# Eight early tile pairs, squares summed beside TensorE, and a new order of the token sums at the start of a feed-forward

## The reference

```python
y = jnp.concatenate([y_a, y_b, y_c, y_d], axis=-1) @ w_out[l]
x = layer_norm(ALPHA * x + g1 * y, ln1_w[l], ln1_b[l])
x = layer_norm(ALPHA * x + g2 * swiglu(x * (1.0 + sc2) + sh2, w_ffn_in[l], w_ffn_out[l]), ln2_w[l], ln2_b[l])

def swiglu(h, w_in, w_out):
    g, u = jnp.split(h @ w_in, 2, axis=-1)
    return (jax.nn.silu(g) * u) @ w_out
```

## Time and profile before

| | us |
|---|---|
| median of 3 runs | 2479.55 (2476.06 to 2481.32) |
| profiled execution | 2475.26 |
| its span | 2473.5 |
| TensorE busy | 2289.2 (93%) |
| VectorE busy | 1366.7 (55%) |
| ScalarE busy | 808.6 (33%) |
| GpSimd busy | 286.2 (12%) |

### The profile page before, as it was taken

The page is one execution under the profiler, slowest core; times in us unless marked ns, Lnnn a source line. Parts: engine busy times, 40 slices in busy tenths (PEclk is TensorE's granted clock), DMA queues, the critical chain, the costliest instruction groups (busy, mean ns, idle before and its releaser), DMA issues. The chain is left out here.

```text
span 2473.5 us, 26601 instructions
## 1 busy us (share of the span) xinstructions
PE 2289.2 (93%) x10498; PEld 1702.9 (69%) x10498; DVE 1366.7 (55%) x2048; ACT 808.6 (33%) x1359; POOL 286.2 (12%) x230
## 2 busy tenths in 40 slices
PE   6999997878969999999999989998799999898999
PEld 3444853567638888887888668985577977444887
DVE  3779538375776555555456575229646186664310
ACT  3101113533362333333433353334344332344210
POOL 0000000200133233220000000026200000021000
PEclk9999989958979999999999999999899999898999
DMA  7541029105312222225543121000222110102322
GB/s 262 159 130 34 1 58 322 39 1 170 119 34 86 90 83 84 77 73 191 190 129 129 56 86 52 26 1 26 69 65 68 35 42 27 52 19 82 99 79 60
DMA packets 210564, 210.47 MB, mean 85 GB/s; under 512 B 18658, under 2 KB 167450, under 8 KB 209512
## 3 DMA queue, kind: packets, MB, share of 16 engines
q1 hardware_dynamic: 194892, 190.51, 24.5%
q0 software_dynamic: 3664, 12.35, 1.4%
q10 hardware_dynamic: 11884, 5.91, 0.9%
HBM read 167.92 MB, written 39.64 MB: 84 GB/s over the span
## 5 line engine op out<-in xcount | busy, mean ns | idle before, releaser
L2234 PE MATMUL bk_in<-t_part,a 128*128 128x512 f32 x1320 | 313.1, 396 | 29.3 <-DVE t_part L2672 10.5
L2234 PEld LDWEIGHTS bk_in<-t_part,a 128*128 128x128 f32 x1320 | 251.6, 191 | 87.3 <-issue 16.6
L2257 PE MATMUL bk_in<-hid_part,b_part 128*128 128x512 f32 x1056 | 245.8, 394 | 7.0 <-DVE b_part L2568 7.0
L2257 PEld LDWEIGHTS bk_in<-hid_part,b_part 128*128 128x128 f32 x1056 | 200.2, 190 | 51.9 <-DVE b_part L2568 8.7
L991 PE MATMUL fr_ps<-arena,work 128*128 128x512 f32 x384 | 168.5, 600 | 5.0 <-DMA work<-in_w_in 5.0
L4204 PE MATMUL fo_ps<-fo_hi,fo_part 128*128 128x512 f32 x512 | 161.8, 394 | 10.8 <-DVE fo_lo L4248 10.8
L2995 PE MATMUL bk_in<-h_part,sj_part 128*128 128x512 f32 x576 | 136.0, 397 | 6.2 <-DVE h_part L2722 5.1
L991 PEld LDWEIGHTS fr_ps<-arena,work 128*128 128x128 f32 x384 | 73.5, 193 | 96.4 <-issue 91.2
L3437 PE MATMUL aj_ps<-h_part,aj_part 128*128 128x512 f32 x576 | 137.9, 400 | 0.0
L2995 PEld LDWEIGHTS bk_in<-h_part,sj_part 128*128 128x128 f32 x576 | 109.4, 191 | 32.8 <-issue 6.2
L2568 DVE TENSOR_TENSOR b_part<-w_raw,b_part 128x1024 fp32r<-128x1024 f32 x60 | 74.2, 1237 | 96.7 <-ACT b_part L2358 85.2
(11 more groups left out here) (616 smaller groups left out, 3885.5 us busy)
## 6 DMA issues: line engine op xcount, KB each, us to landing
work<-in_w_mod SPq DMA_DIRECT2D x24, 1024.0 KB, 8.1
w_raw<-in_w_ffn_out SPq DMA_DIRECT2D x44, 512.0 KB, 3.8
work<-in_w_in SPq DMA_DIRECT2D x25, 512.0 KB, 3.9
g_raw<-in_w_ffn_in SPq DMA_DIRECT2D x24, 512.0 KB, 3.8
w_raw<-in_w_in SPq DMA_DIRECT2D x20, 512.0 KB, 3.7
w_raw<-in_w_out SPq DMA_DIRECT2D x16, 512.0 KB, 3.9
work<-in_w_out SPq DMA_DIRECT2D x8, 1024.0 KB, 7.1
kept_mix<-work SPq DMA_DIRECT2D x12, 512.0 KB, 2.6
```

The lines of the kernel that those rows point to most:

```text
L2234: mm = pe.matmul(bank, ring[n % 4][a][:, k, :], moving[:, b, k, :], start=(opens and k == 0 and j == 0), stop=(k == HK - 1 and j == 2), sk ...
L2257: mm = pe.matmul(pi[:, m, :], w_part[n % 2][:, a, at:at + P], hid_part[k][:, b, :], start=(k == 0 and j == 0), stop=(k == FT - 1 and j == 2))
```

## The change

1. `EARLY` becomes 8: sixteen products of kinds 1 and 2 come before the others, in the order (1,0), (1,1), (2,0), (1,2), (2,1) and so on. They use three pairs of banks (`early_bank`), and the results of tiles 4 to 7 go into half 1's place in `r` (`q_of`, `sg_of`), once half 1 is written to memory. `kept_r` is twice as long; GpSimd issues four DMAs for half 1 (512 KB each), and SP loads it back in four parts in the output projection (`back1`).
2. The squares of each of the two halves get a buffer of eight (`squares_in`). GpSimd adds the first four (`add_squares`), VectorE the other four (`add_squares_in`), and TensorE multiplies these two sums by ones (`variance_in`) in place of eight squares.
3. Half 0's root, reciprocal and scaling come one or two mixing tiles earlier in the lists of ScalarE and VectorE, and all of `h_lo` comes before the last weight split. VectorE makes the last of half 1's seven feature additions, GpSimd the first six.
4. `t_sums`, `t_hi` and `t_rest` are spread over the steps n = 9 to 21, kind by kind. GpSimd makes the four t sums of kind 4 first, then `sum_4(0)`, then the four of kind 7.
5. At the end of the products there are four staging buffers for hidden values; the first weight piece is loaded into free rows of `r`; the first two pieces of hidden values are split before the last two products, and the second piece of weights in step 157. Stores are split into `store_first` and `store_second`.

```diff
-EARLY = 4
+EARLY = 8
...
-    order = [(kind, p + i) for p in range(0, EARLY, 2) for kind in (1, 2) for i in range(2)]
+    order = [(1, 0)]
+    for p in range(1, EARLY):
+        order += [(1, p), (2, p - 1)]
+    order.append((2, EARLY - 1))
...
+    q_of = lambda p: r[:, (0, 4, 1, 5)[p - 4], cut[1]] if 4 <= p < EARLY else pair[p % 4][:, 0, :]
...
-        if g == 0 and k % 4 >= 2:
-            return acc_last if k % 2 == 0 else gate[:, :]
-        return square[:, k % 2, :]
+        return squares_in[:, k, :] if g < 2 else square[:, k % 2, :]
...
+        early_bank = lambda p: (bank_a, bank_b, bank_c, bank_a)[p // 2](p)
...
-                    elif n < EARLY + 2:
-                        sp.wait_ge(s.lo, split(2, n - 2))
+                    elif n < EARLY + 3:
+                        sp.wait_ge(s.lo, split(2, n - 2 if n < EARLY + 2 else EARLY - 2))
...
+                def add_squares(g):
+                    for k in range(1, HK):
+                        pool.wait_ge(s.squared, KT * g + k + 1)
+                        if k > 1:
+                            pool.wait_ge(s.qa, 3 * g + k - 1)
+                        pool.tensor_tensor(acc_a, square_of(g, 0) if k == 1 else acc_a, square_of(g, k), ALU.add)\
+                            .then_inc(s.qa, 1)
...
+                for k in range(HK):
+                    pool.wait_ge(s.scaled, KT + 2 * k + 2)
+                    pool.dma_start(kept_r[:, k:k + 5:4, cut[1]], r[:, k:k + 5:4, cut[1]]).then_inc(s.x1, 16)
...
+                def variance_in(g):
+                    pe.wait_ge(s.qa, 3 * g + 3)
+                    pe.matmul(pn[:, 1, :], S.ones, acc_a, start=True, stop=False)
+                    pe.wait_ge(s.qb, 3 * g + 3)
+                    pe.matmul(pn[:, 1, :], S.ones, acc_b, start=False, stop=True).then_inc(s.var, 1)
...
                 for n in range(PRODUCTS):
-                    product(n)
-                    if n == 0:
-                        sum_of(1)
-                    if n == 2:
-                        variance(1, range(KT))
+                    product(n, (lambda: sum_of(1)) if n == 0 else (lambda: variance_in(1)) if n == 3 else None)
...
+                        elif p >= 4:
+                            act.wait_ge(s.x1, 128)
+                            act.wait_ge(s.h1, KT)
...
+                    if n == 7:
+                        take(3)
+                        take(2)
+                    if n in (8, 9):
+                        for i in (2 * n - 16, 2 * n - 15):
                             h_second(i)
                             h_second(HK + i)
-                            if i == 0:
-                                take(5)
...
+                        take((5, 4)[n - 8])
...
                     if n == 10:
-                        for i in range(HK):
-                            t_hi(4, i)
+                        take(7)
...
+                    for kind, at in ((6, 11), (5, 12), (4, 14), (7, 18), (3, 19)):
+                        if n == at:
+                            for i in range(HK):
+                                t_hi(kind, i)
...
                 for n in range(FIRST):
                     lo(n, n)
...
+                    if n == 11:
+                        root(0)
+                        inverse(0)
                     if n == 12:
-                        root(0)
-                    if n == 13:
-                        inverse(0)
+                        scale(0, range(0, 4))
...
+                    if n == 10:
+                        add_squares_in(0)
+                    if n == 12:
+                        scale(0, range(4, 8))
                     if n in (13, 14):
-                        scale(0, range(4 * (n - 13), 4 * (n - 12)))
-                    if n == 15:
-                        for k in range(4):
+                        for k in range(4 * (n - 13), 4 * (n - 12)):
                             h_lo(k)
...
                     if n == 3:
                         center(1, 1, range(KT))
-                    if n == 4:
+                        add_squares_in(1)
+                    if n == 6:
                         root(1)
-                    if n == 5:
                         inverse(1)
-                    if n == 6:
-                        scale(1, order1)
+                    if n in (7, 8):
+                        scale(1, order1[4 * (n - 7):4 * (n - 6)])
...
+                    if n in (152, 153):
+                        hid_lo(0, n - 152)
                     if n == PRODUCTS:
-                        lo(FROM_B, 0)
...
+                    if n == 157:
+                        lo_out(1)
```

293 lines of the change are left out of this document (156 added, 137 removed).

## The result

The changed kernel takes 2452.64 us (median; 2449.08 to 2456.75) beside 2477.81 (2475.82 to 2481.32) for the kernel before on the same chip: ratio 0.9897, 95% interval 0.9876 to 0.9919. That is −25.2 us; the forecast said −22.7, with 2457 in a range of 2441 to 2471. The profiled execution took 2454.57 us (span 2452.8).

The account below looks back on a forecast made before the run. TensorE, 93% busy, gains only where it waits, mainly in early products paced by VectorE, and at the products' end. −24.2 + 4 + 2 − 1.1 − 3.4 = −22.7 us gave 2457 us, range 2441 to 2471.

Parts of the forecast that it names:

- Half 0: Mixing tiles of half 1: VectorE paces them, tile 15 ends at 669.5 (664.3 before), tiles 12 to 15 wait.
- are more than used up: Mixing: 5.3 us of TensorE saved on half 0's squares, yet mixing ends at 669.5 instead of 664.3.
- Products 0 to 22: First 23 products: 65.2 us of TensorE work plus 17.0 us of waits, ending 82.2 us after T0, at 751.7.
- Clock, +4: Sparse products between T0 + 36 and T0 + 55: low clock stretches cost 4 us, two of them 5.2.
- Write-back and loads, +2: Half 1's write-back: product 7's copy waits 0 to 3 us, pairs 5 and 6 share DMA engines; 2 us together.
- −1.1: End of products: fetching and splitting hidden pieces ahead removes the 1.09 us wait before one of the last products.
- −3.4: Output projection: third piece starts at 13.4 us in place of 16.84, gaining 3.4 us; bounds 5.9 and 1.
- the walk without penalties: Rival for the whole: clock stays up, loads land as alone; −31 us, 2448, or 2444; chance 0.22.
- between 752 and 758: Sign in TensorE's timeline: the 23rd product ends at 752 to 758 us.
- The pair loads: Rival, odd products 5 to 13: loads take 7.8 us, not 3.8; −9 us, 2471; chance 0.17.
- the early passes: Rival: each of four added passes loses 3 us; −11, 2469; chance 0.08 together with late write-back.
- The clock didn't stay low: Slower rival: clock stays at half from tile 12 until product 16; +18 us, 2497; chance 0.05.

Follow-up runs that it names:

- e5a_splits_back: Changed kernel with hidden pieces and second weights piece split after the last product as before, new load order kept; 2452.13 us, ratio to the kernel before 0.9891.
- e9_three: Changed kernel with half 0's reciprocal after split 12, low parts behind splits 14 and 15, product 4's split ahead of the squares' additions; 2447.20 us.
- e8_dead_work: Changed kernel with four dead multiplications by ones (3.5 us of TensorE work) in the middle of product 7; 2450.04 us, ratio to the kernel before 0.9885.

## Why the prediction was right, and which term was off

The bound was named rightly. TensorE's waits sat in this stretch, VectorE and the loads ended them, and the sum came out 2.5 us from the measurement. That it came out so close is in part luck, since errors of several us cancelled. Its terms:

- *Half 0.* The forecast had mixing end 58.2 us after tile 8's start; it was 57.9, with waits of 4.1, 1.5, 1.75 and 1.75 where 4.8, 2.5, 2.4 and 2.3 were forecast and a low stretch of 1.8 us in tile 12 (7.29 in place of 5.5). GpSimd's additions cost VectorE 4.0 us, as forecast. The sentence that the squares' 5.3 us "are more than used up" holds: the squares alone bring the first product to 50.1, and the new order gives 7.8 back, in which all of h is made.
- *Products 0 to 22.* The walk said 82.2 us; it took 80.7. Product 5 started 17.75 us after the first (18.4 forecast), product 6 23.3 (24.5). Products 12 and 13 were given waits of 0.8 and 3.2; in their place stand the slow products 11 and 12, and product 13 starts 52.4 us after the first where the walk had 54.7. Product 9 waited 0.85 us, where the walk had 0.2.
- *Clock, +4.* This term failed. The forecast had two low stretches between the 36th and the 55th us of the products, and wrote "at most two" among its signs. There were three before the 23rd product's end, and only the last lies there: in tile 12, in product 6 (23 us in) and in products 11 and 12 (44 us in). Each lay ahead of a wait whose end something else set, so the loss was taken out of that wait, and the term was 0 here: tile 13 starts 37.5 us after tile 8 in the changed kernel and in six others, whose rows of tile 12 are 7.07 to 7.98 us long, and product 9 starts 33.9 us after the first product here and 34.0 in e5a_splits_back, where product 6 took 3.00 us. The price came from the earlier trace rows, 2.4 and 2.8 us. The second of those rows has no wait behind it (737.66, then 748.66), but the first has, in the kernel before:

```profile
710.27 0.94 PE L2234 MATMUL bk_in<-t_part,a 128*128 128x512 f32 x3 [1.96 <-DVE t_part L2672]
```

So the step that failed is that a stretch's own extra time was taken for the kernel's loss, without a look at the wait behind it. The price isn't always 0: in e9_three, where none stood behind, about 1.3 of 1.6 us counted. What did cost in the changed kernel was 1.6 us in the output, where no term stood.
- *Write-back and loads, +2.* Half of this did not come: ScalarE's copy of product 7 did not wait. The four parts landed 5.1 us after issue in the median, far from the 8.8 of the earlier trace rows, and the starvation that the Trainium skill, page "SBUF — State Buffer", warns of in its note on the "DVE blocks DMA" trap did not show. The other half did: the load of pair 5, beside the write-back (issued within the window 697 to 701), landed after 5.8 us in place of 3.8, and product 9 waits for it.

```profile
g_raw<-in_w_ffn_in SPq DMA_DIRECT2D x1, 512.0 KB, 5.8
```

It took 5.7 to 5.8 us in all twelve profiles that have this write-back, so it is no chance of one execution. No run left the write-back out, so what these 2 us cost at the 23rd product stays open.
- *End.* −1.1 was −0.2: the wait before a late product did not go (0.87). That product (kind 4 of the last tile) goes into the bank of the product just before it (kind 7), which VectorE must first read out. VectorE now starts on this as soon as that product ends and takes 0.69 us, so 0.2 was all that its list had held, and the sign "no wait before the last product" failed. −3.4 was −3.5.

The forecast for the stretch was thus −18.2 and the measurement −26.0, nearly the walk without penalties (−24.2): 7.8 us off, of which 4 had been added for the clock and 2 for the write-back, and 1.8 lay in the walk itself. One sign failed by this: counted from tile 8's start, the 23rd product ends at 749.9 on the forecast's scale, not between 752 and 758. The total came out close because the profiled total lost 1.6 us in the output, and because the medians differ by less than the landmarks: 25.2 beside 27.95. I can't say where the remaining 2.8 go; unchanged code varies by more than that between executions.

Of the rivals, the walk without penalties came nearest in the stretch. The pair loads do set when products 9, 11 and 13 start, but at the length that the walk gave them and not at the rival's 7.8 us (they took 3.7 to 5.8 here, and in e8_dead_work one of 5.4 in place of 3.7 came with 1.4 us). From product 13 to the 23rd only 0.38 us of waits are left, so the early passes were not held. The clock didn't stay low: it came back within tile 12, whose two halves ran at 0.69 (642 to 646) and 0.89 (646 to 650) on the windows' mean.

## What to carry to other kernels

Before a stall, a slow clock or a late load is priced, look for the wait behind it: if another engine or a load sets that wait's end, the loss is absorbed as far as the wait is long, and if no wait stands there it counts. The same low stretch was free in tile 12 of the changed kernel and cost 1.3 us in tile 13 of another version. In a list written by hand, find where the pacing engine itself stands still, and move work that isn't due yet behind what frees it; here 4.6 us of VectorE's idle time gave 3.4 to 3.9. The same work taken from TensorE was worth all of its time in one order of the program and half in another, so a part's worth is to be read in the kernel in which it ends up.

## What the runs showed of the hardware that I had not expected

- A VectorE instruction with a scalar operand and one tensor input from SBUF is delayed as well beside GpSimd's addition: 1.40 us in place of 0.49. The Trainium skill, page "SBUF — State Buffer", section "Who interferes with whom", lists this kind (`tensor_scalar`) among those that can take the shared ports, when their operands meet its conditions; the two meetings agree, and both vanish where GpSimd's additions are cut to 8 columns.
- The same load of 512 KB, alone in its window, took 5.4 us in one execution and 3.7 in another. Beside a write-back of four times 512 KB the load before it took 5.7 to 5.8 in every one of twelve.
- The same code gave a clock that fell in one execution and stayed up in another: from the third output piece to the feature sum 119.8 to 119.9 us in seven profiles, the kernel before's among them, and 121.3 to 121.5 in six, the changed kernel's among them (122.4 in the kernel with the end of the products put back).
